# Page numbers of a paged key/value cache: read four at a time, key and value pairs asked for in turn

## The reference, cut to what matters

```python
PAST_LEN = 2048; PAGE_SIZE = 128; DEC_BATCH = 8; MOBA_HEADS = 4; HEAD_DIM = 128
# cache_k, cache_v (1, 160, PAGE_SIZE, 4, 128) float32; page_table (8, 16) int32
k_all = jnp.concatenate([past_kv[0], mk], axis=1)   # past_kv: the sample's 16 pages, in the table's order
v_all = jnp.concatenate([past_kv[1], mv], axis=1)
...
gate = jnp.einsum('bhtd,bhnd->bhtn', q, k_mean)      # mean key of each block of 256 positions
_, sel = lax.top_k(gate, 3)                          # three past blocks and the own one are attended to
...
logits = q . k * HEAD_DIM ** -0.5 - slope * dist;  p = softmax(logits);  out = p @ v
```

## Time and profile before

| | |
|---|---|
| median of 3 runs | 1222.13 us (1218.21 to 1226.48) |
| the profiled execution | 1225.72 us, of which the span shown is 1224.0 us |
| granted TensorE clock over the span | 0.945 |
| busy: PE, PEld, DVE, ACT, POOL | 90%, 81%, 57%, 46%, 24% |
| chain that ended last | PE 76%, DVE 8%, ACT 6%, issue 3%, DMA 3%, POOL 2%, SPq 2% |
| key pages (kring), value pages (vring) | 128 and 128 DMAs of 256 KB, 3.5 and 3.4 us to landing |
| paged attention | first key page asked for at 242.2 us, last value page at 527.7 us |

### The profile page before, as it was taken

How to read it: one execution, slowest core, us unless ns; L and a number is a source line. 1 busy time by engine, 2 the same in 40 slices (tenths; PEclk the granted TensorE clock), 3 DMA queues, 4 the chain that set the end, 5 groups by cost and what they waited for, 6 DMA issues and landing times.

```text
span 1224.0 us, 20259 instructions
## 1 busy us (share of the span) xinstructions
PE 1105.7 (90%) x7015; PEld 994.8 (81%) x7015; DVE 695.6 (57%) x1192; ACT 563.3 (46%) x886; POOL 289.3 (24%) x274
## 2 busy tenths in 40 slices
PE   5999879976889989887999999988999799999995
PEld 4999778755556656566999999988999699999993
DVE  4843534545776766645666664345664666665333
ACT  3437501234566666545544443445333744543424
POOL 8400113310566666603200000213003300000101
PEclk9989959969899999978999999998999899999997
DMA  7334200055788988662444443443445244453411
GB/s 223 124 119 143 69 1 1 17 186 159 263 272 283 298 287 280 212 213 69 137 137 137 158 166 140 130 138 104 169 140 147 70 137 137 159 169 135 144 52 43
DMA packets 119123, 182.60 MB, mean 149 GB/s; under 512 B 6128, under 2 KB 59471, under 8 KB 118990
## 3 DMA queue, kind: packets, MB, share of 16 engines
q1 hardware_dynamic: 116274, 173.30, 43.4%
q0 software_dynamic: 2784, 8.47, 2.3%
HBM read 176.12 MB, written 5.63 MB: 148 GB/s over the span
## 4 chain that ended last, share of the span: by engine, by line
PE 76%; DVE 8%; ACT 6%; issue 3%; DMA 3%; POOL 2%; SPq 2%; DVEq 0%; ACTq 0%; POOLq 0%
PE bank L1648 70%; PE bank L1942 3%; DMA kring<-cache_k 2%; ACT hi L701 1%; SPq L420 1%; DVE xres L1100 1%; DVE kTl L1100 1%; ACT xres L985 1%; POOL xl L644 1%; DVE lo L1093 1%; SPq L418 1%; PE bank L1658 1%; POOL lo L617 1%; DMA xtok<-x_sample 1%; PE bank L2058 0%
## 5 line engine op out<-in xcount | busy, mean ns | idle before, releaser
L1648 PE MATMUL bank<-xh,hi 128*128 128x320 f32 x1184 | 373.3, 315 | 30.8 <-POOL xl L644 25.1
L1648 PE MATMUL bank<-xl,hi 128*128 128x320 f32 x1184 | 370.9, 313 | 0.0
L1648 PE MATMUL bank<-xh,lo 128*128 128x320 f32 x1184 | 370.6, 313 | 0.0
L1093 DVE TENSOR_TENSOR lo<-raw,hi 128x2048 fp32r<-128x2048 f32 x102 | 242.2, 2375 | 187.9 <-ACT hi L701 187.9
L1648 PEld LDWEIGHTS bank<-xh,hi 128*128 128x128 f32 x1184 | 227.1, 192 | 33.5 <-issue 29.6
L701 ACT ACTIVATE hi<-raw 128x2048 fp32r (+1 forms) x102 | 194.7, 1909 | 107.6 <-PE bank L1648 107.6
L1648 PEld LDWEIGHTS bank<-xl,hi 128*128 128x128 f32 x1184 | 227.2, 192 | 0.1
L1648 PEld LDWEIGHTS bank<-xh,lo 128*128 128x128 f32 x1184 | 226.8, 192 | 0.0
L1100 DVE TENSOR_TENSOR kTl<-bank,kTh 128x512 fp32r<-128x512 f32 x128 | 88.0, 689 | 81.8 <-ACT kTh L701 80.4
L1648 PE MATMUL bank<-hh,hi 128*128 128x320 f32 x416 | 129.5, 311 | 1.3 <-DVE hraw L1100 1.3
L1648 PE MATMUL bank<-hh,lo 128*128 128x320 f32 x416 | 128.6, 309 | 0.0
(11 more groups left out here) (388 smaller groups left out, 1503.3 us busy)
## 6 DMA issues: line engine op xcount, KB each, us to landing
raw<-w_up SPq DMA_DIRECT2D x44, 1024.0 KB
kring<-cache_k SPq DMA_DIRECT2D x128, 256.0 KB, 3.5
vring<-cache_v SPq DMA_DIRECT2D x128, 256.0 KB, 3.4
raw<-w_down SPq DMA_DIRECT2D x8, 2048.0 KB
raw<-w_in_mix SPq DMA_DIRECT2D x7, 2048.0 KB
raw<-w_in_sc SPq DMA_DIRECT2D x8, 1024.0 KB
raw<-w_down SPq DMA_DIRECT2D x4, 1536.0 KB
raw<-w_out_mix SPq DMA_DIRECT2D x2, 2048.0 KB
```

Of the source, the lines that this page charges most:

```text
L1093: dve.tensor_tensor(lo[:, p], weight(n)[:, :, 256 * p:256 * p + 256], hi[:, p], ALU.subtract)\
L1648: return pe.matmul(out, lhsT, rhs, start=start, stop=stop, **kw)
```

## The change

`pair` and the step `pages` go. At the head of a round, `load_list(n)` brings the four numbers `ptab[4n:4n+4]` into four registers of SP with a range check (0 to 159) on each, and `listed` keeps them: the key pages of round n use them at once, the value pages of the same numbers five rounds later. The list stands ahead of the wait for the key ring. Within a round the order is now: key pair, value pair, key pair, value pair. In round 5 the wait for `po1` stands ahead of the list and the keys. SP waits for the table itself in place of `pages`.

```diff
-            DV.wait(sp_, "pages")
+            sp_.wait_ge(s["pt_in"], 16)
+            listed = {}
+
+            def load_list(n):
+                _, x = nc.values_load_multi_w_load_instructions(ptab[0:1, 4 * n:4 * n + 4], engines=[sp_.engine], min_val=0,
+                                                                max_val=POOL - 1)
+                for i in range(4):
+                    listed[4 * n + i] = x[i]
 
             def load_pair(out, cache, landed, n):
-                w = sp_.value_load(pair[0:1, n:n + 1], min_val=0, max_val=POOL * POOL - 1)
-                for u, x in enumerate((w % POOL, w // POOL)):
+                for u in range(2):
+                    x = listed[2 * n + u]
                     sp_.dma_start(out[:, u, :], cache[bass.ds(x, 1)].rearrange("o p h d -> (o p) (h d)")).then_inc(s[landed], 16)
 
             for n in range(4 * NB + 5):
@@
-                if n < 4 * NB:
-                    after(sp_, "kT_mm", 4 * n - 4)
-                    x = (n + 1) % 2
-                    load_pair(kring[:, x, 0:2], a["cache_k"][0], f"k_in{x}", 2 * n)
-                    load_pair(kring[:, x, 2:4], a["cache_k"][0], f"k_in{x}", 2 * n + 1)
                 if n == 5:
                     PE.wait(sp_, "po1")
-                for m in (2 * n - 10, 2 * n - 9):
+                for i, m in enumerate((2 * n - 10, 2 * n - 9)):
+                    if n < 4 * NB:
+                        x = (n + 1) % 2
+                        if i == 0:
+                            load_list(n)
+                            after(sp_, "kT_mm", 4 * n - 4)
+                        load_pair(kring[:, x, 2 * i:2 * i + 2], a["cache_k"][0], f"k_in{x}", 2 * n + i)
                     if m >= 0:
                         after(sp_, "v_lo", m - 3)
                         load_pair(vring[:, m % 4], a["cache_v"][0], f"v_in{m % 4}", m)
+                        listed.pop(2 * m), listed.pop(2 * m + 1)
@@
-            dve.wait_ge(s["pt_in"], 16)
-            two = ptab[:, :].rearrange("o (a u) -> o a u", u=2)
-            DV.up(dve.scalar_tensor_tensor(out=pair[:, :], in0=two[:, :, 1], scalar=float(POOL), in1=two[:, :, 0],
-                                           op0=ALU.mult, op1=ALU.add), "pages")
```

More of the change, by code:

```diff
@@ L118 @@
     "dve": """
-gz pages xres0 xres1 xres2 xres3 xres4 xres5 xres6 xres7 xl0 xl1 xl2 xl3 xl4 xl5 xl6 xl7 ba gxa gx gone beta gsp g ug0
+gz xres0 xres1 xres2 xres3 xres4 xres5 xres6 xres7 xl0 xl1 xl2 xl3 xl4 xl5 xl6 xl7 ba gxa gx gone beta gsp g ug0
 qknorm qkn gcl0 cumsb0 dmax0 dmat0 ug1 mask0 La0 intra0 L0 tok0 qg0 gcl1 cumsb1 dmax1 dmat1 ug2 mask1 La1 intra1 L1
@@ L165, in trunk_program @@
         ptab = sb("ptab", [1, NB * NPG], I32)
-        pair = sb("pair", [1, NB * NPG // 2], I32)
         ones = sb("ones", [P, P])
```

## The result

The changed kernel takes 1232.03 us in the median of 9 runs (1226.49 to 1237.58), the kernel before 1221.13 (9 runs on the same chip). The ratio is 1.0086, 95% interval 1.0067 to 1.0106: some 10.5 us slower. Run again beside other kernels it was 1.0098 (1.0075 to 1.0121).

The account below looks back on a forecast made before the run. It took SP's wait for a value slot, with the next key round queued behind, to make keys late. Slot chain +4.8, clock +2.3 and round five +0.5 gave +7.6 on 1222.1: 1230 us, range 1215 to 1240.

Parts of the forecast that it names:

- What bounds it: Late key pages in paged attention: SP waits for a value slot behind which the next key round is queued; 11.2 us.
- Loads and checks: SP, each round: one load and four checks take 1.39 us instead of 2.28; a round falls from 6.77 to 5.83.
- rival C: SP's list load is paid by the number, the list takes 2.3 us, total 1238 us; chance 0.14.
- Flight: Last key page's DMA on the chain stays 4.07 us in flight, though six pages go out 0.555 us apart.
- The rounds between: Rounds between the six late ones gain 0.94 us of SP's time each, which buys nothing; they land in time.
- six waits of 2.2 us and more: Sign of the forecast: TensorE waits six times for key pages, 2.2 us and more each.
- the slot chain: From freed value slot to last key issue: 5.5 us instead of 4.7, +0.8 a batch, six times +4.8.
- Clock: TensorE drops to half speed after longer key waits: two new dips of 1.15 us each, +2.3; ends 0 and 4.6.
- Round five: SP's wait for the prompt's last matmul now precedes the keys; nearly 4 us late, mostly covered by VectorE: +0.5 us.
- Rival D: Round five isn't covered, VectorE queues behind late transpositions; with the forecast's longer slot chain 1233 us; chance 0.12.
- B: Rival, faster: SP's rate sets key arrival, 0.94 us a round makes keys punctual; 1208.6 us, half 1215; chance 0.15.
- E: Rival: nothing moves, quicker flight of the denser pages takes back the 0.8 us; 1220 to 1224 us; chance 0.21.

Follow-up runs that it names:

- five-slot pair: A fifth slot for value tiles added to the kernel before and to the changed kernel: 0.997 and 1.002 of the kernel before.
- the doubled list: The changed kernel with each round's list loaded and checked twice: 1.0205 of the kernel before.
- second profile: Both kernels run again unchanged and profiled: executions of 1221.17 us (before) and 1227.87 us (changed); timed ratios 1.0002 and 1.0098.

## Why the prediction was right or wrong

*What bounds it* held. The five-slot pair shows it for the kernel before, not only from the chain: with the wait for the slot gone, the late rounds shrink to about half.

*Loads and checks* held: 0.301 us for four numbers, 1.36 for the list against 1.39 forecast and 2.3 in rival C, which falls. Three more registers cost 0.03 us in the row of the changed kernel. The Trainium skill's "Runtime: NRT & Kernel Launch", section "Instruction fetch mechanics", has about 200 ns for each, for loads from HBM; the loads of this kernel, from `ptab`, don't cost that. (The prediction's sum with a load of 0.6 us was added up wrong: it gives +0.2 a batch, not +0.1.) Address arithmetic, costed at nothing, shrank for keys to 0.042 us, and for values it is gone altogether: 0.52 us a key page and 0.47 a value page instead of 0.555. That is why the chain took 5.2 and not 5.5 us.

*Flight* was mis-sized. I kept it at 4.07 us on the ground that six pages 0.555 apart don't pile up. They are 0.47 to 0.52 apart, and the last key page took 4.6 and 5.3 us. It is so in all rounds: from 355 to 490 us the last key page of a round is in flight 3.9 us in the median in both profiles of the kernel before, where the last six pages take 3.9 us or more to issue, and 4.8 in both of the changed one, where it is mostly 2.5 to 2.8. With the new order and the old loads both are 3.9 again, and with the old order and the list ahead, the last six issued in mostly 2.5 to 3.8 us, it is 4.8; so the length comes with the closer requests and not with the order. On the chain above the smaller issue time and the longer flight make 9.9 us from slot to TensorE, where 9.6 were forecast.

*The rounds between* failed as written. I said that they land in time now and that the middle value pair's slot was free within a tenth or two. It came free 0.27 us after the key pair before it, the second key pair stood behind it, the flight grew, and a second round of each batch was late (0.18 to 1.59 us in the first profile, 0.59 to 0.77 in the second). The sign that was to show the forecast, six waits of 2.2 us and more, did not come either: behind round five the longest was 2.11 us in the first profile and 2.30 in the second, and each batch's lateness is split over two rounds. That 0.79 us a batch were measured where 0.8 were forecast is therefore partly luck: three parts were off, the issuing by less, the flight and the second late round by more. Whether a small wait is absorbed by the slot chain, as the sentence has it, no run tested alone; the doubled list shows that a larger one is not.

*Clock.* The price of a dip is from rows, but the point from which one comes was not there to be read. In the second profile of the kernel before a wait of 2.41 us kept full clock, and in the changed one 2.17 and 2.30 did; in its first profile stretches at half clock began after 2.11, 2.01 and 1.99 us (columns as in the earlier trace rows):

```profile
329.80:333.20 3.40, 3.40 (x17) 2.17 (x16) 0.69 (x1) 1.09 (x2) 2.23 (x1) 0.51 0.95 310
459.50:462.90 3.40, 3.40 (x13) 2.32 (x12) 2.33 (x9) 2.14 (x4) 2.28 (x1) 0.51 0.91 332
490.30:493.70 3.40, 3.40 (x14) 2.53 (x13) 2.48 (x11) 2.30 (x3) 2.38 (x1) 0.50 0.97 333
```

The price itself was a little high: by the same subtraction the full-clock batches of the second profile before take 27.1 to 27.3 us, not 26.9, which makes a dip 0.8 to 1.1 us. What the runs leave is 6.7 us between two executions at full clock in the keys' part, of which 1.2 were there before the late rounds (at unit 28), and 10.5 to 12 between the medians. That most of the rest is dips can be estimated, since the granted clock of every timed run is on record. On the chip of the second profiles its mean is 0.9455 in the changed kernel (6 runs) and 0.9495 in the kernel before (31 runs). With half clock and full clock as the only levels that is some 134 us at half clock against 123, 11 us more or some three dips of 3.4 us: by 0.8 to 1.15 us each an estimated 2.4 to 3.5 us of time, where 2.3 were forecast. Where in the timed runs they fall is not seen.

*Round five.* Issue at 300.35 for the first page and TensorE at 307.43, against 301.6 and 307.9 forecast. VectorE took that unit at 309.28, before 310.38, so the cover was there, and by the 22.1 us from unit 16 to unit 28, before and after, the move cost nothing, not 0.5. Rival D falls.

*Total*: +7.6 forecast, 1230; 1232.03 measured, +10.5 by the ratio. Added up anew: 0.79 for six batches, 4.7; dips, 2.4 to 3.5; round five, nothing. That leaves 2 to 3.5 us of the 10.5 without a named place. B, the only way to be faster, lost: SP's rate was not what made the keys late. E lost too: the denser pages fly longer, not quicker.

## What to carry to other kernels

Ask of a queue what it waits for, not how long its instructions take: issuing time saved behind a wait on a freed buffer, and then spent in front of the next one, is worth little, and anything put behind that wait is paid: the doubled list cost as much as ten or eleven rounds of it in full. Two streams of requests in one queue should stand so that the one that is needed next is never behind a slot or the pages of the other; preparation that waits for nothing (here the list) belongs ahead of the wait, though with the old order this was not worth a measurable amount. And before pricing the removal of a wait, look which engine would be late right behind it: here 11 us of waits were worth 4.

## What the runs showed of the hardware that was not expected

A register load of four numbers costs 0.301 us against 0.267 for one. The last key page of a round, 128 rows of 2 KB, lands 4.8 us after its issue in the median when the last six pages are issued in mostly 2.5 to 2.8 us, against 3.9 when their issue takes 3.9 us or more. And whether TensorE is granted half clock after an idle of about 2 us is not told by the length of that idle alone: 2.41 us kept full speed in one execution, 1.99 lost it in another.
